# Scores of a prompt attention branch, two heads at a time in the two row halves of the array

## The reference

```python
h = x * (1 + sc1) + sh1
qa, ka, va, qb, kb, vb, ga, gb = jnp.split(h @ w_in, W_IN_SPLITS, axis=-1)
...
# first branch: 3 groups (window, dilation) = (128,1), (512,4), (2048,16), 4 heads of 64 in each
s = jnp.einsum('bghnqe,bghnke->bghnqk', qb, kk) * (E ** -0.5)     # masked to window and stride
p, lse = _softmax_lse(jnp.where(valid, s, -jnp.inf))
...
# the three groups of a head are merged by their softmax denominators
w = jax.nn.softmax(jnp.stack(lses, axis=0), axis=0)
...
# second branch: 4 heads, causal in the own block of 256 keys
merged = (jax.nn.sigmoid(ga) * (oa @ w_pa) + jax.nn.sigmoid(gb) * (ob @ w_pb))
x = _layer_norm(ALPHA * x + g1 * (merged @ w_o), ln1_g, ln1_b)
```

## Time and profile before

| | us |
|---|---|
| runs of the kernel before | 570.11, 570.53, 572.04 |
| median | 570.53 |
| the profiled execution's own time | 575.18 |
| its span, first to last instruction | 573.6 |
| PE busy | 526.1 (92%) |
| DVE busy | 290.2 (51%) |
| ACT busy | 224.3 (39%) |
| mean granted TensorE clock | 0.942 |

### The profile page before, as it was taken

The page is one execution under the profiler, slowest core; times in us unless marked ns, Lnnn a source line. Parts: engine busy times, 40 slices in busy tenths (PEclk is TensorE's granted clock), DMA queues, the critical chain, the costliest instruction groups (busy, mean ns, idle before and its releaser), DMA issues.

```text
span 573.6 us, 10305 instructions
## 1 busy us (share of the span) xinstructions
PE 526.1 (92%) x4047; PEld 482.0 (84%) x4047; DVE 290.2 (51%) x560; ACT 224.3 (39%) x376; POOL 92.4 (16%) x127
## 2 busy tenths in 40 slices
PE   4677999999998999999999979999999999999990
PEld 2446899989876889888689969999999999999990
DVE  0064647556634434334387576645455555345356
ACT  1043333334334354435543346465444343333321
POOL 1000113002850000000044250911111100000005
PEclk9657799999999699999999989999999999999995
DMA  8997599988087692065534460799876674364102
GB/s 282 327 284 229 185 365 335 347 280 269 12 280 207 216 324 80 1 190 184 188 106 147 149 215 27 258 351 332 270 262 225 217 251 147 113 218 148 36 1 82
DMA packets 96718, 116.70 MB, mean 203 GB/s; under 512 B 3595, under 2 KB 87755, under 8 KB 96164
## 3 DMA queue, kind: packets, MB, share of 16 engines
q1 hardware_dynamic: 94788, 102.67, 55.4%
q0 software_dynamic: 1888, 13.44, 6.7%
HBM read 112.82 MB, written 13.57 MB: 220 GB/s over the span
## 4 chain that ended last, share of the span: by engine, by line
PE 76%; DMA 9%; DVE 4%; SPq 3%; ACT 3%; issue 2%; POOL 2%; POOLq 0%; DVEq 0%; ACTq 0%
PE psum L618 20%; PE psum L620 19%; PE psum L619 19%; DMA raw<-in_w_in 6%; PE psum L643 3%; PE psum L821 2%; DMA raw<-in_w_ada 2%; PE psum L850 2%; PE psum L739 2%; PE psum L651 2%; PE psum L836 1%; DVE w_lo L434 1%; PE psum L808 1%; PE psum L925 1%; SPq L521 1%
## 5 line engine op out<-in xcount | busy, mean ns | idle before, releaser
L618 PE MATMUL psum<-act_hi,w_hi 128*128 128x288 f32 x736 | 225.4, 306 | 9.5 <-DVE act_lo L1575 3.5
L434 DVE TENSOR_TENSOR w_lo<-raw,w_hi 128x1024 fp32r<-128x1024 f32 x118 | 146.7, 1244 | 170.0 <-ACT w_hi L429 169.8
L619 PE MATMUL psum<-act_lo,w_hi 128*128 128x288 f32 x736 | 220.5, 300 | 0.0
L620 PE MATMUL psum<-act_hi,w_lo 128*128 128x288 f32 x736 | 219.5, 298 | 0.0
L429 ACT ACTIVATE w_hi<-raw 128x1024 fp32r<-128x1024 f32 x118 | 124.1, 1056 | 138.2 <-PE psum L620 92.4
L618 PEld LDWEIGHTS psum<-act_hi,w_hi 128*128 128x128 f32 x736 | 141.4, 192 | 18.0 <-issue 10.5
L620 PEld LDWEIGHTS psum<-act_hi,w_lo 128*128 128x128 f32 x736 | 141.8, 193 | 0.0
L619 PEld LDWEIGHTS psum<-act_lo,w_hi 128*128 128x128 f32 x736 | 141.7, 193 | 0.2
L618 PE MATMUL psum<-f_hi,w_hi 128*128 128x288 f32 x176 | 52.4, 298 | 0.6 <-DVE f_t L1613 0.6
L619 PE MATMUL psum<-f_lo,w_hi 128*128 128x288 f32 x176 | 51.9, 295 | 0.0
L620 PE MATMUL psum<-f_hi,w_lo 128*128 128x288 f32 x176 | 51.8, 294 | 0.0
(11 more groups left out here) (180 smaller groups left out, 570.7 us busy)
## 6 DMA issues: line engine op xcount, KB each, us to landing
raw<-in_w_ada SPq DMA_DIRECT2D x24, 1024.0 KB, 7.2
raw<-in_w_up SPq DMA_DIRECT2D x22, 1024.0 KB, 6.4
raw<-in_w_in SPq DMA_DIRECT2D x19, 1024.0 KB, 7.2
raw<-in_w_down SPq DMA_DIRECT2D x10, 1024.0 KB, 5.0
out<-in_cache_kv_a POOLq DMA_DIRECT2D x16, 504.0 KB, 6.1
raw<-in_w_o SPq DMA_DIRECT2D x4, 1024.0 KB, 5.0
kvin<-in_cache_kv_a SPq DMA_DIRECT2D x8, 256.0 KB, 3.8
kvin<-in_cache_kv_b SPq DMA_DIRECT2D x16, 128.0 KB, 3.6
```

The source lines that it names most:

```text
L434: nc.vector.tensor_tensor(part(w_lo, slot4, by_rows), raw_half(rslot, hh, by_rows), part(w_hi, slot4, by_rows).bitcast(F32), ALU.subtract) ...
L618: nc.tensor.matmul(out, hi_l, hi_r, start=start, stop=False, skip_group_check=True)
L619: nc.tensor.matmul(out, hi_l, lo_r, start=False, stop=False, skip_group_check=True)
L620: return nc.tensor.matmul(out, lo_l, hi_r, start=False, stop=stop, skip_group_check=True)
```

## The change

Scores of the first branch are computed for two heads (u and u + 1) at once, in stages 2, 4, 6 and 8; stages 3, 5, 7 and 9 have no scores. The six matmuls alternate between the upper and the lower row half. The scores of a pair for t = 1 take 1536 columns, that is three banks (2, 3, 4) in place of two; the middle bank is shared by both heads. PE waits on its own semaphore `half_bank` between the two matmuls that write the middle bank from different halves. The odd head has its groups in the order 2, 0, 1, with its own copy of the mask; the constants grow by 128 columns. The turned probabilities move from banks 4, 5 to banks 5, 7 for u < 4 (4, 5 afterwards), those of the samples from banks 4 to 6 to banks 5 to 7. `softmax_max`, exponentials, transposes and values stay one unit to a stage.

```diff
@@ constants @@
-C_MA0 = C_MA1 + 768
+C_MA0 = C_MA1 + 1024
 C_MB1 = C_MA0 + 384
-C_MB0 = C_MB1 + 256
-C_EPS = C_MB0 + 128
+C_EPS = C_MB1 + 256
...
+def scores_of(s):
+
+    if 2 <= s < 10:
+        return (s - 2, s - 1) if s % 2 == 0 else ()
+    return (s - 2,) if 10 <= s < N_UNITS + 2 else ()
+
+def scored_by(u):
+
+    return u // 2 + 1 if u < 8 else u - 3
+
+def groups_of(u):
+
+    br, t, _ = UNITS[u]
+    return (3,) if br else (2, 0, 1) if t and u % 2 else (0, 1, 2)
+
+def score_col(u, i):
+
+    br, t, _ = UNITS[u]
+    return (768 if t else 512) * (u % 2) if br == 0 else 512 * i
+
+def turn_banks(u):
+    return (5, 7) if u < 4 else (4, 5)
...
+    half_bank = sem("half_bank")
@@ tensor engine @@
-        def prompt_scores(u):
...
+        def score(u, i, n):
             br, t, heads = UNITS[u]
+            h, nk = heads[i], 128 * (t + 1)
+            g, p0, c0 = groups_of(u)[n], E * (h % 2), score_col(u, i) + nk * n
+            return nc.tensor.matmul(psum[:, 2 + c0 // 512, c0 % 512:c0 % 512 + nk],
...
+        def prompt_scores(us):
+            if us[0] >= 1:
+                pe.wait_ge(maxed, rows_before(us[0]))
+            u = us[0]
+            if u < 4:
+                score(u, 0, 2).then_inc(half_bank, 1)
+                score(u + 1, 0, 1)
+                score(u, 0, 0)
+                pe.wait_ge(half_bank, u // 2 + 1)
+                score(u + 1, 0, 0)
+                score(u, 0, 1)
+                mm = score(u + 1, 0, 2)
+            elif u < 8:
+                for n in range(3):
+                    score(u, 0, n)
+                    mm = score(u + 1, 0, n)
+            else:
+                for i in range(2):
+                    mm = score(u, i, 0)
             mm.then_inc(scored, 1)
@@ stage loop @@
             if s == 2:
                 pe.wait_ge(max_s, 2)
-                prompt_scores(0)
+                prompt_scores(scores_of(s))
                 sample_probs_turn()
-            if 3 <= s < N_UNITS + 2:
-                prompt_scores(s - 2)
+            elif scores_of(s):
+                prompt_scores(scores_of(s))
@@ vector engine @@
-            dve.wait_ge(scored, u + 1)
+            dve.wait_ge(scored, scored_by(u))
```

More of the change, by code:

```diff
@@ L128, in constants @@
     for g in range(3):
-        c[:, C_MA1 + 256 * g:C_MA1 + 256 * (g + 1)] = prompt_mask(1, g)
+        c[:, C_MA1 + 256 + 256 * g:C_MA1 + 256 + 256 * (g + 1)] = prompt_mask(1, g)
         c[:, C_MA0 + 128 * g:C_MA0 + 128 * (g + 1)] = prompt_mask(0, g)
     c[:, C_MB1:C_MB1 + 256] = prompt_mask(1, 3)
-    c[:, C_MB0:C_MB0 + 128] = prompt_mask(0, 3)
+    c[:, C_MA1:C_MA1 + 256] = prompt_mask(1, 2)
     c[:, C_EPS] = EPS
@@ L237, in cols_of, with mask_col @@
     return keys_of(u) * len(UNITS[u][2])
+def scores_of(s):
[10 more added lines that the diff above has]
+    return (768 if t else 512) * (u % 2) if br == 0 else 512 * i
+def mask_col(u):
+    br, t, _ = UNITS[u]
+    if br == 0:
+        return (C_MA1 + (0 if u % 2 else 256)) if t else C_MA0
+    return C_MB1 if t else C_MB1 + 128
+def turn_banks(u):
+    return (5, 7) if u < 4 else (4, 5)
 def build(nc, x_prompt, x_sample, cache_a, cache_rows, cache_b, page_table, c_prompt, c_sample, w_ada, b_ada, w_in,
@@ L789, in sample_probs_turn @@
             for n, (c0, nc_) in enumerate(S_PIECES):
-                mm = nc.tensor.transpose(psum[0:nc_, 4 + n // 4, 128 * (n % 4):128 * (n % 4) + 128],
+                mm = nc.tensor.transpose(psum[0:nc_, 5 + n // 4, 128 * (n % 4):128 * (n % 4) + 128],
                                          s_prb[:, c0:c0 + nc_], ident)
@@ L811, in sample_values @@
             mm.then_inc(pv_s, 1)
-        def prompt_scores(u):
+        def score(u, i, n):
             br, t, heads = UNITS[u]
[L815 to L825, removed]
+            h, nk = heads[i], 128 * (t + 1)
+            g, p0, c0 = groups_of(u)[n], E * (h % 2), score_col(u, i) + nk * n
+            return nc.tensor.matmul(psum[:, 2 + c0 // 512, c0 % 512:c0 % 512 + nk],
+                                    qkvg[p0:p0 + E, q_blk(g, h // 2), 128 * t:128 * t + 128],
+                                    qkvg[p0:p0 + E, k_blk(g, h // 2), 0:nk], start=True, stop=True, skip_group_check=True)
+        def prompt_scores(us):
[17 more added lines that the diff above has]
+                    mm = score(u, i, 0)
             mm.then_inc(scored, 1)
@@ L845, in prompt_values @@
                 pe.wait_ge(o_ready, u)
-            groups, n = (0, 1, 2) if br == 0 else (3,), 0
+            groups, n = groups_of(u), 0
             for i, h in enumerate(heads):
@@ L1137, in prbT_copy @@
             n = min(512, cols_of(u))
-            nc.scalar.activation(prbT[:, u % 2, 0:n], psum[:, 4, 0:n], ACT.Copy).then_inc(prbT_a, 1)
+            nc.scalar.activation(prbT[:, u % 2, 0:n], psum[:, turn_banks(u)[0], 0:n], ACT.Copy).then_inc(prbT_a, 1)
         def sigmoids(c0, c1):
@@ L1444, in softmax_max @@
                 dve.wait_ge(exped, rows_before(u))
-            n, m0 = keys_of(u), ((C_MA0, C_MA1), (C_MB0, C_MB1))[br][t]
+            n, m0 = keys_of(u), mask_col(u)
             for i in range(len(heads)):
                 r = rows_before(u) + i
-                src = psum[:, 2:4, :].rearrange("p b c -> p (b c)")[:, 512 * i:512 * i + n]
+                src = psum[:, 2:5, :].rearrange("p b c -> p (b c)")[:, score_col(u, i):score_col(u, i) + n]
                 link(V.tensor_tensor_reduce(msk[:, i * n:i * n + n], src, cst[:, m0:m0 + n], 1.0, -3.0e38, ALU.add, ALU.max,
@@ L1458, in prbT_copy @@
                     dve.wait_ge(pv_done, u - 1)
-                V.tensor_copy(prbT[:, u % 2, 512:n], psum[:, 5, 0:n - 512]).then_inc(prbT_b, 1)
+                V.tensor_copy(prbT[:, u % 2, 512:n], psum[:, turn_banks(u)[1], 0:n - 512]).then_inc(prbT_b, 1)
         def out_copy(u):
@@ L1475, in own_rows @@
             if half == 0:
-                dve.wait_ge(scored, 8)
+                dve.wait_ge(scored, scored_by(7))
             pick = cst[:, C_SELM + 4 * half:C_SELM + 4 * half + 4].unsqueeze(2).broadcast_to([128, 4, E])
```

4 lines of the change are left out of this document (2 added, 2 removed).

## The result

Over 22 runs each, the changed kernel takes 564.85 us in the median (562.38 to 570.11), the kernel before 570.46 (564.86 to 574.16). The ratio is 0.993 with a 95% interval of 0.991 to 0.995, which is 4.0 us less (2.9 to 5.1). The forecast was 3.5 us less, 567.0 us, with 565.7 to 569.3 as the range. The two medians by themselves lie further apart, 5.6 us; I go by the ratio, which comes with an interval and puts the changed kernel at 566.5.

What follows compares the result with a forecast made beforehand. The prediction took PE to bound the attention part and summed 0.6 (stage 3) - 0.3 (second pair's wait) + 3.36 (stages 5, 7, 9) - 0.2 (masks) = 3.5 us less, 567.0 us, range 565.7 to 569.3.

Steps and rivals of the forecast that it cites:

- What bounds the part: Attention part: PE bounds it, so PE time taken out of a stage is worth itself until ACT or DVE is later.
- What two heads at once cost: Score pairs: six matmuls alternating between row halves take as long as three in one half, 1.56 and 0.93 us.
- rival 1: Score pairs: the halves overlap only in part, so each pair loses a pass; 567.4 us; chance 0.13.
- rival 3: Score pairs: no overlap in a long row, blocks of 2.85 and 1.59 us; 569.5 us; chance 0.09.
- rival 4: Score pairs: each change of row half empties the array, at 0.2 us each; 573.5 us, slower; chance 0.05.
- PE's wait for itself: Pairs of t = 1: the fourth matmul waits for the first, costing 0.32 us a pair, bounds 0 and 0.65.
- Stage 3: Without scores, transposes of u = 0 wait for the exponential: PE idle some 0.6 us, 0.6 us gained.
- Stages 5, 7, 9: These stages lose their score blocks and gain them in full: 1.54 + 0.91 + 0.91 = 3.36 us.
- Masks: Constants' load grows by 65 KB while the DMA engines are saturated: 0.18 us lost, bounds 0 and 0.2.
- Rival 2: Stages 3 and 4: ACT and DVE set the pace, copies or splits 1 us later; 568.0 us; chance 0.09.
- Rival 5: Stage 3's new hole: the clock falls, a 6.7 us low stretch costing 3.4 us; 570.5 us; chance 0.04.
- My sign for a failure: Ahead of the changed part: a difference already there at 200 us would show the prediction wrong.

Runs made afterwards that it cites:

- before_load_first: Kernel before the change, with the late gate weight's load issued earlier on SP, ahead of the third sequence's cached values; 568.78 us, ratio to before 0.9980.
- exp_first: Changed kernel, in stage 2 ACT's exponential and DVE's row maximum of u = 0 put before the late gate weight's split; 562.43 us, ratio to before 0.9865.
- before_again: Kernel before the change, unedited, run for a second profile; 568.10 us, ratio to before 1.0004.
- after_again: Changed kernel, unedited, run for a second profile and time; 565.98 us, ratio to before 0.9957.
- late_wait: Changed kernel with the half_bank wait and the odd head's matmul into the shared bank moved last in the pair; 566.07 us, ratio to before 0.9970.
- apart: Changed kernel with a pair's matmuls not alternating, three of one head and then three of the other; 567.65 us, ratio to before 0.9968.
- pair_first_tile: Changed kernel with pairs for u = 4 to 7 alone, single heads for u = 0 to 3; 567.79 us, ratio to before 0.9953.
- the second measurement: The unedited changed kernel timed again (after_again); 565.98 us, ratio 0.9957 against runs of the kernel before with median 568.81 us.
- both: Changed kernel with the edits of exp_first and late_wait together; 562.45 us, ratio to before 0.9853.
- before_exp_first: Kernel before the change, with the turned stage 2 order of exp_first on ACT and DVE; 568.10 us, ratio to before 0.9975.

## Why the prediction was right, step by step

The distances of the transposes from the first scores show where each piece comes from, first without a hole (before_load_first, exp_first), then with one (before_again, after_again):

| transposes of u | 0 | 1 | 2 | 3 | 4 | 5 | 6 | 7 |
|---|---|---|---|---|---|---|---|---|
| before_load_first | 7.42 | 12.90 | 19.72 | 25.91 | 32.10 | 37.98 | 48.23 | 53.19 |
| exp_first | 6.16 | 11.93 | 17.17 | 23.32 | 28.56 | 34.38 | 43.69 | 48.61 |
| less by | 1.26 | 0.97 | 2.55 | 2.59 | 3.54 | 3.60 | 4.54 | 4.58 |
| before_again | 8.89 | 14.37 | 21.19 | 27.38 | 33.58 | 39.45 | 49.70 | 54.67 |
| after_again | 7.64 | 13.44 | 18.69 | 24.84 | 30.08 | 35.90 | 45.21 | 50.13 |
| less by | 1.25 | 0.93 | 2.50 | 2.54 | 3.50 | 3.55 | 4.49 | 4.54 |

- **What bounds the part: PE.** Right. Each skipped block comes back in full at the next transposes, and nothing is given back later: from the end of the part to the long run of gate-sized matmuls near 330 us it is 63.0 us in all profiles of this study but one, with and without the change; the first profile after has 63.6, and in it the clock is low from 269.4 to 272.8 us, just behind the part (last section).
- **What two heads at once cost: what one costs.** Right: 1.57 us without the wait (late_wait), 0.94 for t = 0. Rivals 1, 3 and 4 fall; apart shows that two heads issued one behind the other overlap too, so rival 3 needs more than a bad order. The rule of the Trainium skill that was weighed there ("TensorE: Matmul & The Clock Gate", Part 2, matmuls stay in program order) does not describe what was measured: in apart a row of the other half started ahead of three rows that stand before it.
- **PE's wait for itself: 0.32 us.** Right: 0.31, and 0.29 in the step from u = 0 to u = 1 without a hole.
- **Stage 3: a hole of 0.6 us, and 0.6 us gained.** This is the term that was mis-sized. The path to the transposes was right to the hundredth (4.56 us from the landing in five traces), but I had taken the landing's place relative to PE from one execution in which it was 2.24 us behind the first scores. In six others of this order it was 2.78 to 4.58, and the hole 1.33 to 2.60. In pair_first_tile, where a low clock ahead of the part held up PE as in the first trace (first scores at 198.69), it was 1.72, and there was no hole. I had also not seen that the kernel before then has a hole of its own. With a late weight the step is worth 3.44 + 1.49 - 4.56 = 0.37 us (the other 0.87 of the 1.25 is the weight that landed 3.09 instead of 3.96 us behind the scores). Without one it is worth 1.58 - 0.32 = 1.26.
- **Stages 5, 7, 9: 3.36 us.** Right and a little low: 1.58 + 0.95 + 0.94 = 3.47, that is the upper end of each block, and 0.04 to 0.06 more at each unit behind.
- **Masks: 0.2 us lost.** Not settled. The first scores begin anywhere between 191.1 and 198.7 us in the profiles other than the first; 0.2 us can't be seen in that. A larger constant load was not run, so this term stays argued.
- **The sum.** With a late weight 0.37 - 0.32 + 3.47 + 0.14 = 3.66 us, measured 4.54 - 0.87 = 3.67; without a hole on either side 4.6. The 3.5 were closer to the first. The measured 4.0 (2.9 to 5.1) admits both; the 2.4 of the second measurement (0.5 to 4.3, from 0.9957 of 568.81) admits the first and not quite the second. That the sum came out this near is in part luck: its 0.6 for stage 3 was 0.2 too much for a late weight and 0.7 too little for one in time, and its 0.2 for the masks no run shows.
- **Rivals 2 and 5.** Rival 2's mechanism, a late weight, is what happened, but its price was wrong: stage 4 lost nothing, because its maximum hangs on the same landing and keeps its distance, and the kernel before pays for the late weight as well. Rival 5 happened in one kernel, apart, at 1.5 us, not 3.4. My sign for a failure, a difference that is there at 200 us, was in the first pair of profiles and meant nothing for the change: the earlier trace rows show the low clock in it.

**The best version.** Four kernels with the pairs and (almost) without the wait for the late weight have medians of 562.3 to 562.9 us, of six runs each, and ratios of 0.985 to 0.990; the change has 0.993 and 0.9957. The interval of `both`, [0.9804, 0.9901], lies below that of the change, [0.991, 0.995]; those of the other three touch it. The reordering alone gives 0.9975 and 0.9980, and neither can be told from 1. In the part, the hole costs the change 1.5 to 2.2 us and the kernel before 1.5 in the one profile that has it; what else lies between the medians the part does not explain. Among the four these times allow no choice.

## What to carry to other kernels

Where matmuls use only half of the array's rows, issue two independent ones in turn, one in either half, and if two of them share a bank and one waits for the other, as here, put the wait in front of the last: the second head was free, and the wait cost 0.3 us only while something was queued behind it. Whether the shared bank needs that wait no run shows; every kernel with pairs of t = 1 has it. Before you price the removal of PE work, look for the transfer that anchors the stage and take a second execution: a chain that hangs on a landing keeps its distance from the landing and not from PE, and a slow stretch of PE can hide it. Then move what does not need the transfer ahead of what does, on the engine that serves both.

## What the runs showed of the hardware beyond that

The order of the program did not hold between the row halves. In apart the odd head's first row started 0.54 us after the block, together with the even head's third, and its six rows then ran beside the rest; how far ahead PE can reach in this way was not tried.

The clock can fall without any hole. Stretches of before_exp_first, PE busy all through in the samples' values:

```profile
230.00:237.50 7.50, 7.50 (x52) 6.66 (x51) 3.70 (x12) 2.80 (x6) 0.00 (x0) 1.00 0.01 2
237.70:241.00 3.30, 3.30 (x32) 1.03 (x26) 0.00 (x0) 0.52 (x3) 0.00 (x0) 0.50 0.00 0
```

In the second stretch the matmuls use 32 columns of the array (L808) and the granted clock is 0.50, 1.2 GHz, with no idle PE ahead of it. The same code ran at the upper clock in the other profiles, so this costs 1.6 us in some executions and nothing in others. `both` has such a fall, for 3.4 us and at a cost of 1.6, in the same loop in stage 13 (L844 there). The first profile after has one from 269.4 us on, in other matmuls of 32 columns (L679), 2.6 us behind a hole of 0.29.

A hole of one length does not always have a fall behind it either. In the place of the new hole, the clock fell behind 2.60 us and did not behind 2.08. Ahead of the part, where the first trace has a hole of 1.96 us and a low clock behind it, `both` has one of 1.95 us that ends at 182.91, and before_load_first one of 1.39 that ends at 182.30. Stretches behind these two, first of both, then of before_load_first:

```profile
183.00:196.00 13.00, 13.00 (x121) 11.32 (x122) 7.32 (x18) 6.35 (x11) 0.00 (x0) 1.00 0.87 277
```

```profile
184.40:191.20 6.80, 6.80 (x53) 5.44 (x53) 1.73 (x7) 1.70 (x2) 0.00 (x0) 0.50 0.97 325
```

Rival 5 was built on two rows, this one and the hole of 3.51 us further back. This one does not repeat: in these two profiles the longer hole kept the upper clock and the shorter one did not. The other does: behind the hole of 3.5 us the clock fell in all fourteen profiles, for 6.8 us in eleven and for 3.4 in three (after, late_wait, pair_first_tile). What decides these runs don't say.
